# A decoder layer on one core: expert weights asked for in whole blocks instead of halves, and five smaller moves around it

## What is computed

```python
h = rms_norm(x, mix_norm_g[l]) * (1.0 + scale_m) + shift_m
mix = mixer_sublayer(h, w_in[l], ...)
x = x + gate_m * mix
h = rms_norm(x, ffn_norm_g[l]) * (1.0 + scale_f) + shift_f
...
a = einsum('td,edf->tef', tc, w1);  b = einsum('td,edf->tef', tc, w3)
hid = silu(a) * b * gates[:, :, None]
routed = einsum('tef,efd->td', hid, w2)
...
x = x + gate_f * (routed + shared)
return rms_norm(x, final_norm_g)
```

## Time and profile before

| | before |
|---|---|
| median of three executions | 780.43 us |
| the profiled execution | 779.75 us |
| span from its first to its last instruction | 776.9 us |
| TensorE, matmuls | 724.5 us, 93% of the span |
| TensorE, loads of its stationary side | 382.4 us, 49% |
| VectorE | 324.8 us, 42% |
| ScalarE | 173.6 us, 22% |
| the sync engine's DMA queue | 264.27 MB, 88.4% of 16 DMA engines' span |
| all reads from memory | 269.62 MB |

### The profile page before, as it was taken

The page is one execution under the profiler, slowest core; times in us unless marked ns, Lnnn a source line. Parts: engine busy times, 40 slices in busy tenths (PEclk is TensorE's granted clock), DMA queues, the critical chain, the costliest instruction groups (busy, mean ns, idle before and its releaser), DMA issues.

```text
span 776.9 us, 12706 instructions
## 1 busy us (share of the span) xinstructions
PE 724.5 (93%) x5002; PEld 382.4 (49%) x5002; DVE 324.8 (42%) x812; ACT 173.6 (22%) x347; POOL 8.7 (1%) x22
## 2 busy tenths in 40 slices
PE   4699999999999999999999999899999989898985
PEld 1388888888886444343333333333343333333322
DVE  1108693855556485333234333331333233222325
ACT  3213320200000333222122222221222122112213
POOL 0200001000000000000000000000000000000000
PEclk9999999999999999999999999999999999999998
DMA  9999726695959497999999999999999999999991
GB/s 338 378 349 365 226 84 227 234 308 182 337 198 412 185 342 286 411 416 411 414 412 411 414 414 411 412 414 413 412 413 414 410 412 414 413 413 412 412 376 70
DMA packets 91715, 271.44 MB, mean 349 GB/s; under 512 B 6456, under 2 KB 35264, under 8 KB 82832
## 3 DMA queue, kind: packets, MB, share of 16 engines
q1 hardware_dynamic: 89952, 264.27, 88.4%
q0 software_dynamic: 1408, 6.31, 2.2%
q10 hardware_dynamic: 304, 0.13, 0.1%
HBM read 269.62 MB, written 1.05 MB: 348 GB/s over the span
## 4 chain that ended last, share of the span: by engine, by line
PE 55%; SPq 27%; DMA 7%; DVE 5%; issue 3%; ACT 2%; DVEq 0%; ACTq 0%
PE bank L1126 54%; SPq L368 20%; SPq L373 5%; DMA ring<-exp_w_dram 5%; DMA ring<-ada_w_dram 2%; SPq L364 2%; DVE slot_gate L1062 1%; PE bank L1468 1%; DVE reg L1066 1%; DVE reg L1057 1%; ACT reg L640 1%; DMA reg<-reg 1%; DVE h_hT L1117 0%; DVE bank L1080 0%; DVE reg L963 0%
## 5 line engine op out<-in xcount | busy, mean ns | idle before, releaser
L1126 PE MATMUL bank<-ring,h_hT 128*32 128x512 f32 (+2 forms) x2112 | 259.3, 590 | 16.2 <-DMA ring<-exp_w_dram 16.2
L1126 PEld LDWEIGHTS bank<-ring,h_hT 128*32 128x32 f32 (+1 forms) x2112 | 83.3, 114 | 174.8 <-issue 141.6
L1126 PE MATMUL bank<-h_hT,ring 128*128 128x256 f32 x704 | 155.6, 380 | 1.8 <-ACT h_hT L484 1.8
L1126 PEld LDWEIGHTS bank<-h_hT,ring 128*128 128x128 f32 x704 | 133.3, 190 | 20.9 <-ACT h_hT L484 2.0
L1126 PE MATMUL bank<-ring,const_misc 128*32 128x512 f32 x1008 | 116.5, 595 | 0.3
L1057 DVE TENSOR_TENSOR reg<-reg,bank 128x256 f32<-128x256 f32 x32 | 13.5, 421 | 186.7 <-ACT reg L640 186.7
L1080 DVE TENSOR_TENSOR bank<-bank,reg 128x512 f32<-128x512 f32 x64 | 44.5, 695 | 54.5 <-PE bank L1126 54.5
L1084 DVE TENSOR_TENSOR y_part<-bank,y_part 128x512 fp32r<-128x512 f32 x64 | 44.3, 692 | 42.5 <-ACT y_part L651 21.3
L1126 PEld LDWEIGHTS bank<-ring,const_misc 128*32 128x32 f32 x1008 | 30.2, 109 | 61.7 <-issue 57.3
L640 ACT ACTIVATE reg<-bank 128x256 f32<-128x256 f32 x32 | 12.3, 386 | 197.9 <-PE bank L1126 197.9
L1126 PE MATMUL bank<-take,h_part 128*128 128x256 f32 x288 | 50.1, 298 | 0.5 <-ACT h_hT L625 0.5
(11 more groups left out here) (232 smaller groups left out, 445.1 us busy)
## 6 DMA issues: line engine op xcount, KB each, us to landing
ring<-exp_w_dram SPq DMA_DIRECT2D x252, 512.0 KB, 15.3
ring<-exp_w_dram SPq DMA_DIRECT2D x63, 1024.0 KB, 15.7
ring<-ada_w_dram SPq DMA_DIRECT2D x24, 1024.0 KB, 12.8
ring<-w_in_dram SPq DMA_DIRECT2D x24, 1024.0 KB, 12.4
ring<-w_branch_dram SPq DMA_DIRECT2D x4, 1024.0 KB, 12.8
ring<-w_out_dram SPq DMA_DIRECT2D x4, 1024.0 KB, 8.1
ring<-shared_w_dram SPq DMA_DIRECT2D x2, 1024.0 KB, 15.4
spare<-exp_w_dram SPq DMA_DIRECT2D x2, 1024.0 KB, 14.9
```

The lines of the kernel that those rows point to most:

```text
L1126: return pe.matmul(o, lhsT, rhs, start=start, stop=stop, skip_group_check=True)
```

## The change

- **Whole blocks.** w13 of a pair is one DMA of 1 MB for each slot, rows of 8 KB, all four issued when `w13_used` says that pair n - 2 is through k = 7. TensorE waits for all four before k = 0.
- **Halves stay for four pairs and the spare's:** pair 2 (low halves at `w13_half`, high ones at `w13_used`) and the last pair of each body (7, 15, 23, 31). For these last the low halves still come first, so that TensorE can begin on them, but both are asked for at `w13_used`.
- **A third half slot.** The region of `scale_f`, free after h2, takes the high half of w1 of pair 7's second expert. That half is not loaded with pair 7. For k = 4 to 7 that expert's products are two of 256 columns instead of one of 512.
- **Order of requests.** The new half and the first half of the spare w2 go ahead of pair 1's w2 loads; the second half of the spare w2 goes between the low and the high halves of pair 2.
- **`final_g`** goes to slot 0 of the ring, issued by SyncE at the end, after `w13_used` of pair 30.
- **Gates.** The product with `turner` and its waits move to between k = 3 and k = 4 of the same pair (ahead of k = 7 in pair 0), and VectorE's four sums go ahead of `th`.
- **The start.** `columns(2)` goes ahead of `ada(6)`. Unit 0 is split by k: k = 0 to 3 for both halves of the outputs after `h_done` 4, k = 4 to 7 after `h_done` 8; its upper half goes to bank 4, and ScalarE reads it in two sigmoids. `keep_busy` puts six products of 256 columns, whose result is not used, between the `ada` and `columns` groups.

```diff
+LOW, HIGH = slice(0, UNIT // 2), slice(UNIT // 2, UNIT)
-        final_g = scale_f
+        final_g = ring[:, 0, 0:D]
+        spare_w1 = scale_f.rearrange("p (k f) -> p k f", f=FF)
...
-            def load_step(use, it, spared=False):
-
-                for r in range(RING_PAIRS):
-                    for h in range(2):
-                        sp.wait_ge([w13_half, w13_used][h][r], use)
-                        for e in range(spared and r == SPARE_PAIR % 2, 2):
-                            for w in range(2):
-                                load_13(r, e, w, h, it)
-                    sp.wait_ge(w2_used[r], use)
-                    for e in range(spared and r == SPARE_PAIR % 2, 2):
-                        load_2(r, e, it)
+            def load_pair(r, use, it, halves, first_e=0):
+
+                if isinstance(use, int) and halves and use == 1:
+                    sp.wait_ge(w13_half, 1)
+                else:
+                    sp.wait_ge(w13_used[r], use)
+                for cols in ((LOW, HIGH) if halves else (slice(0, UNIT),)):
+                    if isinstance(use, int) and use == 1 and cols == HIGH:
+                        load_spare_half(1)
+                        sp.wait_ge(w13_used[r], use)
+                    for e in range(first_e, 2):
+                        for w in range(first_e if cols == HIGH else 0, 2):
+                            load_13(r, e, w, it, cols)
+                sp.wait_ge(w2_used[r], use)
+                for e in range(first_e, 2):
+                    load_2(r, e, it)
...
+                    sp.wait_ge(S["h2_done"], TB)
+                    sp.dma_start(scale_f, w13_src[0][2 * SPARE_PAIR + 1][:, HIGH]).then_inc(spare_landed, 16)
+                    load_spare_half(0)
                 for e in range(2):
                     sp.wait_ge(*used_up(LAST[6 * r + 4 + e]))
                     load_2(r, e, 0)
-            for j in range(2):
-                sp.wait_ge(*[(S["picked_done"], TB), (S["pair_gates"], 1)][j])
-                sp.dma_start(spare_half[j], w2_src[2 * SPARE_PAIR][:, j * D:(j + 1) * D]).then_inc(spare_landed, 16)
...
+            sp.wait_ge(w13_used[0], passes * STEPS)
+            sp.dma_start(final_g, a["final_norm_g"].rearrange("(o d) -> o d", o=1).partition_broadcast(P)).then_inc(S["final_in"], 16)
...
-            pool.wait_ge(S["h2_done"], TB)
-            pool.dma_start(final_g, a["final_norm_g"].rearrange("(o d) -> o d", o=1).partition_broadcast(P))\
-                .then_inc(S["final_in"], 16)
...
+            def keep_busy(count):
+
+                pe.wait_ge(S["ac_done"], 1)
+                for i in range(count):
+                    mm(bank[0][:, 256:512], ident, x_sb[:, 0, 0:256])
...
             ada(5)
+            keep_busy(1)
+            columns(2)
             ada(6)
-            columns(2)
+            keep_busy(3)
             ada(7)
+            keep_busy(1)
             columns(3)
+            keep_busy(1)
...
-            pe.wait_ge(S["h_done"], 8)
-            channels(0, ("mix", 0))
+            pe.wait_ge(S["h_done"], KD // 2)
+            w = begin_unit(0, ("mix", 0))[1]
+            for half in range(2):
+                if half:
+                    pe.wait_ge(S["h_done"], KD)
+                for m in range(2):
+                    for k in range(half * (KD // 2), (half + 1) * (KD // 2)):
+                        ins = mm(bank[B_UNIT_0[m]][:, 0:T], w[:, k, m * P:(m + 1) * P], hT[:, k, :], k == 0, k == KD - 1)
+            ins.then_inc(S["unit_done"], 1)
...
+            def pair_turned(before, n, r, parity, gm):
+
+                if before:
+                    pe.wait_ge(S["y_low"], n)
+                pe.wait_ge(S["pair_gates"], n + 1)
+                mm(bank[B_Y[0]][:, 0:P + 8], take[:, parity, gm, :, :], turner[:, r, :]).then_inc(S["gate_mm"], 1)
...
+                    halves = m == BODY_PAIRS - 1 or isinstance(use, int) and n == 2
...
                     for k in range(KD):
-                        if k % (KD // 2) == 0:
-                            pe.wait_ge(w13_landed[r][k // (KD // 2)], step * 64 + (32 if late else 64))
+                        if k == 0 and halves:
+                            pe.wait_ge(w13_low[r], use * 64 + 32 if m == SPARE_PAIR else 64)
+                        if k == (KD - 1 if first else KD // 2):
+                            pair_turned(not first, n, r, parity, gm)
+                        if k == (KD // 2 if halves else 0):
+                            pe.wait_ge(w13_landed[r], step * 64 + (16 if late else 64))
```

## The result

The changed kernel took 773.71 us, the median of four executions (772.38 to 774.05), beside 780.35 us (778.43 to 783.27) for the kernel before: a ratio of 0.9909, 95% interval 0.9886 to 0.9931. That is 6.6 us less, not the 11.0 of the forecast; it lies inside the range and nearest to rival 2's 774, and rival 2's late requests are what the runs show.

A forecast was written before the change was run, and what follows sets the result against it. DMA waits on TensorE until about 290 us, then full DMA sets the end from about 310. Terms -1.3 - 1.75 + 0.35 - 1.27 + 1.2 - 9.2 + 1.0 = -11.0 gave 768.8, median 769.5; range 765 to 778.5.

The forecast's parts named there:

- rival 2: Part of the gain lost to late requests, or a later end: 3 to 5 us of the 11, so 774; chance 0.22.
- The gap at 292 us: Idle DMA before pair 1's w2: two loads moved in, pair 2 asked for earlier; 1.75 us off.
- the end: Last pairs: pair 30 waits for its whole block, making pair 31 late for its high half; 1.0 us on.
- Pair 7, nothing: Pair 7's smaller load saves 1.27 us, but 1.2 is lost waiting for pair 8's request, put at 385.2.
- the start: Mixer's unit 0 starts at 31.0 instead of 32.32, held by its weights, and TensorE carries that through; 1.3 us off.
- pair 3's request: Pair 3's w13 asked for at `w13_used` of pair 1, at 318.2, data at 319.4; 0.35 us on.
- the gates: Moved ahead: 0.7 us less waiting in pair 0, 0.27 us in each pair from pair 1; moving `turner` costs nothing.
- The rate: Full DMA stretch: 8 KB rows at 422 against 407 GB/s, 0.37 us a pair over 25 pairs; 9.2 us off.
- `keep_busy`: Six idle products at the start stand in waits and give nothing, as the clock is already up; 0.22 us each.

The follow-up runs named there:

- the repeated profile: The changed kernel run once more, with nothing altered, beside the kernel before: 772.81 us, ratio 0.9899.

## Why the prediction was right in sign and kind, and wrong in size

**Right.** What bounds the kernel: DMA to the end, with a rate that goes by the row's length. The full stretch was forecast at 418 to 421 GB/s and is at 419. Pair 31 doesn't wait between k = 3 and k = 4. Pair 2 is asked for right after k = 3 of pair 0, and a hole before pair 8 was forecast. The gap at 292 us was to be nearly filled, and is not; the half megabyte went in ahead of it.

**The sum, split at the landing of pair 8's w13.** The last of its four DMAs, issue to landing (minimum, median, maximum), in the kernel after, issued from 388.6 to 390.05:

```profile
DMA to landing us min/median/max: 4.8/8.4/12.1
```

So it is there at 390.05 + 12.1 = 402.2. In the kernel before the last half is issued at 388.84 and takes 13.3, also 402.1. In the repeated profile it is 388.75 + 12.1 = 400.8.

| | forecast | first profile | again |
|---|---|---|---|
| pair 8's w13 landed | -4.6 | 0.0 | -1.3 |
| from there to pair 30, 20 whole pairs | -7.4 | -5.9 | -6.2 |
| the end | +1.0 | +1.3 | +1.3 |
| last w2 products | -11.0 | -4.6 | -6.3 |

(-4.6 are the steps -1.3, -1.75, +0.35, -1.27 and +1.2, and five pairs of 0.37.)

**The step that failed** is the time of pair 8's request, in "Pair 7, nothing". I saw that this request waits for TensorE and put it at 318.2 + 5 x 13.4 = 385.2, less the 1.3 us of the start: 383.9. It came at 387.30 in the repeated run, 3.4 us later, and that is the whole of the 3.3 us by which the first line of the table misses there. From the request to the landing of the last block it is 13.55 us in both profiles of the changed kernel. Of the 3.4 us, 1.3 are the start's; 0.9 are pair 3's request, at 319.09 and not 318.2, since the 0.7 us that the gates were to save aren't there; and 1.2 are five pairs of 13.64 us (319.09 to 387.30) instead of 13.4. In the first profile the later start adds 1.3 more. The kernel before had the number: its high halves of pair 8 go at the same step of TensorE, k = 7 of pair 6, from the same start of pair 0, and are issued from

```profile
L368 SPq DMA_DIRECT2D ring<-exp_w_dram x4: 332/357/383, 387.4 to 388.8; - x4
```

on. The request is a cap: what the DMA gains ahead of it, pair 2 earlier (1.75), the whole rows of pairs 3 to 6 (1.5), pair 7's smaller load (1.27), cannot pass it. By my sum the DMA was done at 385.2, and the cap took 1.2 us of that; at 387.3, with data at 388.5, it takes 3.3. The holes show it: 1.4 and 2.0 us of missing work before pair 3 in the two profiles (274 and 205 GB/s from 318 to 322 us, against 420), forecast at 0.35, and 1.5 and 1.7 before pair 8, forecast at 1.2. The 1.3 us that the repeated profile shows at pair 8 are what could be gained up to the cap; the kernel before had no hole there. This is rival 2, to which I gave 0.22.

**The start** was forecast at -1.3 and gave +1.3 in the first profile and 0.0 in the repeated one. The step that failed is the landing of unit 0's weights, 31.0, taken from the pace of the `ada` units (it was 32.4). It lies ahead of TensorE's 91.8 us, and was, with the gates, the only term that could have moved the cap.

**The rate** was mis-sized. I took 422 against 407 GB/s from stretches of 2 to 6 us, 0.37 us a pair; 20 pairs gave 5.9 and 6.2, or 0.30 to 0.31. The rule that I had set beside it (the Trainium skill, "DMA: Bandwidth & Descriptors", "Why small descriptors are slow (HBM only)") gives 0.12 a pair by an estimate of 1.1%. The traces do not agree, it is too small by more than half: 411 against 422 GB/s with rows of 4 and of 8 KB are 2.7%.

**The gates** were to save 0.27 us of waiting in each pair. The wait is gone (transposes at 322.06 have none), but the `turner` product amid w13 opens a pause of its own: k = 4 starts at 316.69, 3.81 after k = 0, where 32 products without it take 3.45 (744.55 to 748.00); behind k = 7, before, it took 0.17. A pair takes 13.61 us (312.88 to 326.49) instead of 13.66. Most of it was slack either way, but I had also counted on it for the request of pair 8.

**`keep_busy`** was to give nothing in this execution, as the clock was at its upper level already. Its sum is near nothing, but for another reason: without it the clock fell in the changed order (0.55), and with it the fetch falls where unit 0's weights are under way. In the profile of the kernel before with whole blocks, which has no idle products, the clock was at 0.78 from 27 to 33 us. So that start, too, falls in some executions, and one profile could not show it.

**The end** was forecast at +1.0 and is +1.3. `final_g` cost nothing.

## What to carry to other kernels

In a ring of two, ask for each stretch who makes the next request. If the other engine does, then its time from the start of the stretch is a cap: read that time from the trace of the kernel before, where the same step stands in it, compare it with the *sum* of all that is saved ahead of it, and count only what either moves that engine or lies behind the last hole. Where two stages meet, halves at the edge (here pairs 3 and 8) make the hole smaller, though part of it can move on to the next whole block, and whole blocks behind it give the rate.

## What the runs showed of the hardware that was not expected

- Rows of 4 KB instead of 8 KB moved 411 instead of 422 GB/s in a full queue, and after a hole 252 instead of 322 over 7 us. In that kernel the DMA's lateness came back enlarged: one wait of TensorE of 2.31 us, with its clock at 0.50 behind it, put the next request off by 4.2 us.
- One 16 KB fetch of instructions goes to one of the 16 DMA engines and takes 1.1 us there. Where it came at 28.8 to 29.5 us, a load that needs all 16 took 17.5 to 18.0 us to land, and 16.4 to 16.5 where it came later: 1.0 to 1.6 us more, though the mean rate of the stretch shows nothing (349 to 354 GB/s from 27 to 33 us).
- The granted clock at the start fell to 0.55 in the changed order with no idle products, held 1.00 with six of 256 columns in all eight profiles, and fell to 0.76 after 33 us in both with three of 512, 512 and 256. The number of idle columns (1536 and 1280) was nearly the same. In the old order, without idle products, it held 1.00 in two profiles and was at 0.78 in a third.
